# Token rows of a mixture of experts: split once ahead of all pairs of experts, instead of once in every pair

## The reference, cut to what matters

```
u2 = modulate(rmsnorm(h, g_norm2), sh2, sc2)          # 256 x 1024 token rows
comb = weights of the 2 experts (of 32) chosen for each token, zero elsewhere
for e in range(32):
    hid = silu(u2 @ w1[e]) * (u2 @ w3[e])             # 1024 -> 512
    y = y + comb[:, e] * (hid @ w2[e])                # 512 -> 1024
```

## Time and profile before

| | us |
|---|---|
| median of 3 executions | 2202.26 |
| lowest, highest | 2196.2, 2210.37 |
| the profiled execution | 2203.71 |
| its span, first to last instruction | 2201.9 |

### The profile page before, as it was taken

One profiled execution on the slowest core, in us unless ns is written; L12 is line 12 of the kernel. 1 busy time (PEld: TensorE's weight loads), 2 busy tenths in 40 slices (PEclk: granted clock), 3 DMA queues, 4 the chain that ended last, 5 costly groups with the idle time before them and its releaser, 6 DMA issues. The chain is left out here.

```text
span 2201.9 us, 34859 instructions
## 1 busy us (share of the span) xinstructions
PE 2115.3 (96%) x13433; PEld 1839.4 (84%) x13433; DVE 1655.9 (75%) x2247; ACT 1111.8 (50%) x1291; POOL 455.8 (21%) x239
## 2 busy tenths in 40 slices
PE   6999999999999999999999998999979999999996
PEld 6998999559998998999658997999957777777775
DVE  5665887548666765778538655788789999999998
ACT  4343353334433433354324343524348888888885
POOL 8600180809004500081718100000010000000000
PEclk9999999999998999999999999999989999999999
DMA  8854564436655655464336653435649999999994
GB/s 260 267 183 141 158 213 141 143 125 226 211 176 186 232 184 178 145 200 154 134 134 211 199 193 96 153 116 166 235 155 362 369 369 378 364 362 377 367 366 171
DMA packets 238996, 484.33 MB, mean 220 GB/s; under 512 B 10612, under 2 KB 178848, under 8 KB 222528
## 3 DMA queue, kind: packets, MB, share of 16 engines
q1 hardware_dynamic: 226880, 443.58, 57.5%
q0 software_dynamic: 11424, 37.44, 5.1%
q10 hardware_dynamic: 608, 2.14, 0.2%
HBM read 482.03 MB, written 1.09 MB: 219 GB/s over the span
## 5 line engine op out<-in xcount | busy, mean ns | idle before, releaser
L748 PE MATMUL misc<-xh,ring_low 128*128 128x256 f32 x1536 | 427.9, 279 | 0.0
L747 PE MATMUL misc<-xl,high_b 128*128 128x256 f32 x1408 | 394.0, 280 | 9.4 <-DVE xl L2117 6.9
L749 PE MATMUL misc<-xh,high_b 128*128 128x256 f32 x1408 | 392.0, 278 | 0.0
L748 PEld LDWEIGHTS misc<-xh,ring_low 128*128 128x128 f32 x1536 | 291.9, 190 | 3.4
L2779 DVE TENSOR_TENSOR ring_low<-ring,high_b 128x2048 fp32r<-128x2048 f32 x128 | 287.1, 2284 | 0.0
L747 PEld LDWEIGHTS misc<-xl,high_b 128*128 128x128 f32 x1408 | 267.2, 190 | 13.7 <-DVE xl L2117 7.1
L749 PEld LDWEIGHTS misc<-xh,high_b 128*128 128x128 f32 x1408 | 267.0, 190 | 0.0
L2126 DVE TENSOR_TENSOR ring_low<-ring,high_b 128x2048 fp32r<-128x2048 f32 x88 | 226.2, 2611 | 39.7 <-ACT high_b L1613 39.7
L1890 ACT ACTIVATE high_b<-ring 128x2048 fp32r<-128x2048 f32 x124 | 235.7, 1914 | 33.9 <-DMA ring<-in_w_dram 33.0
L1644 ACT ACTIVATE arena<-arena 128x256 f32<-128x256 f32 x88 | 36.8, 418 | 427.7 <-DVE arena L2160 427.7
L1310 PE MATMUL misc<-high_b,ue 128*128 128x512 f32 x512 | 204.2, 399 | 1.9 <-DVE ue L2822 1.2
(11 more groups left out here) (426 smaller groups left out, 4964.1 us busy)
## 6 DMA issues: line engine op xcount, KB each, us to landing
ring<-in_w_dram SPq DMA_DIRECT2D x128, 1024.0 KB, 7.8
ring<-in_w_in_dram SPq DMA_DIRECT2D x72, 1024.0 KB, 5.5
ring_d<-in_w_dram SPq DMA_DIRECT2D x128, 512.0 KB, 5.2
ring<-in_ffn_w_gate_dram SPq DMA_DIRECT2D x44, 1024.0 KB, 5.4
ring<-in_ffn_w_up_dram SPq DMA_DIRECT2D x44, 1024.0 KB, 7.8
ring_d<-in_ffn_w_down_dram SPq DMA_DIRECT2D x88, 512.0 KB, 7.3
arena<-in_w_ada_dram POOLq DMA_DIRECT2D x48, 512.0 KB, 4.4
ring<-in_w_out_dram SPq DMA_DIRECT2D x20, 1024.0 KB, 4.9
```

Source lines behind the costliest of these rows:

```text
L747: pe.matmul(dst, wh, ml, start=start, stop=False, **kw)
L748: pe.matmul(dst, wl, mh, start=False, stop=False, **kw)
L749: return pe.matmul(dst, wh, mh, start=False, stop=stop, **kw)
```

## The change

The rows `u2` are split into `uh` and `ul` (fp32r, in the room of `xh` and `xl`) once ahead of the loop: ACT copies `uh` between its second and third block of weights, DVE subtracts `ul` after the first choice. `sel` becomes fp32r. The gather makes for each group two passes, with `uh` and with `ul` (a pair then has 32 fp32r matmuls of 128 columns), and the two results lie beside each other in one bank of 512 columns, in the order that `ue` has. So a group is moved to `ue` by one copy of 512 columns: for q = 0, 1 by ACT, for q = 2, 3 by DVE, and that copy drains the bank. In a pair's orders, ACT's `high(i + 1, 0, 0)` comes behind `gate3` instead of ahead of the tokens, and DVE has nothing between the `low_d` and `hidden_e` 1. `u2` now lies in the room of `y2`.

```diff
 def gather(i, groups, before=0):                                # PE
-    for q in groups:
-        b = claim3(i, TOKENS[q] - before)
-        for kk in range(2):
-            k = 2 * q + kk
-            for t in range(NT):
-                mm = pe.matmul(b[:, kk * P:(kk + 1) * P], u2[:, t, k * P:(k + 1) * P], sel[:, t, :], ...)
-        mm.then_inc(filled, 1)
+    banks = {}
+    for part_, rows_ in enumerate((uh, ul)):
+        if before and part_ and groups[0] == 0:
+            pe.wait_ge(ul_ready, NT)
+        for q in groups:
+            if not part_:
+                banks[q] = claim3(i, TOKENS[q] - before)
+            b = banks[q].rearrange("p (k h s c) -> p k s h c", k=2, h=2, s=2)
+            for kk in range(2):
+                k = 2 * q + kk
+                for t in range(NT):
+                    mm = pe.matmul(b[:, kk, part_], rows_[:, t, k * P:(k + 1) * P],
+                                   sel[:, t, :].rearrange("p (h c) -> p h c", h=2), ...)
+            if part_:
+                mm.then_inc(filled, 1)
...
 def tokens(i, groups, turn_=0):                                 # ACT
     for q in groups:
         wait_pair_filled(act, i, F_TOKENS[q] if turn_ == 0 else q - 3)
-        act.activation(ue[:, 2 * q:2 * q + 2, :, 0:CAP], bank_of(M0 + TOKENS[q])[:, 0:2 * P]...,
-                       ACT.Copy).then_inc(ue_high, 1)
+        act.activation(ue[:, 2 * q:2 * q + 2, :, :]..., bank_of(M0 + TOKENS[q]),
+                       ACT.Copy).then_inc(drained[(M0 + TOKENS[q]) % 4], 1)
...
 def from_down(i, last):                                         # ACT
     products(i, 1, 7)
+    tokens(i, (0, 1))
+    gate3(i, 1)
     if not last:
         high(i + 1, 0, 0)
-    tokens(i, range(2))
-    gate3(i, 1)
-    tokens(i, range(2, 4))
...
 def tokens(i, groups):                                          # DVE
     for q in groups:
-        dve.wait_ge(ue_high, i * 4 + (4 + q + 1))
-        dve.tensor_tensor(ue[:, 2 * q:2 * q + 2, :, CAP:2 * CAP], bank_of(M0 + j)[:, 0:2 * P]...,
-                          ue[:, 2 * q:2 * q + 2, :, 0:CAP].bitcast(F32), ALU.subtract)...
+        wait_pair_filled(dve, i, F_TOKENS[q])
+        dve.tensor_copy(ue[:, 2 * q:2 * q + 2, :, :]..., bank_of(M0 + TOKENS[q]))\
+            .then_inc(drained[(M0 + TOKENS[q]) % 4], 1)
...
 def pair(i, last):                                              # DVE
     for c in range(CPE):
         low_d(i, 1, c)
-    tokens(i, range(2))
     hidden_e(i, 1)
     if not last:
         low(i + 1, 0, 0)
-    tokens(i, range(2, 4))
+    tokens(i, (2, 3))
...
 # ahead of the loop
+    for t in range(NT):                                         # ACT, between blocks x_ = 1 and 2
+        act.wait_ge(u2_rows, t + 1)
+        act.activation(uh[:, t, :], u2[:, t, :], ACT.Copy).then_inc(uh_ready, 1)
 choose(0)                                                       # DVE
+for t in range(NT):
+    dve.wait_ge(uh_ready, t + 1)
+    dve.tensor_tensor(ul[:, t, :], u2[:, t, :], uh[:, t, :].bitcast(F32), ALU.subtract).then_inc(ul_ready, 1)
 weighing()
 weigh(0, 0)
-tokens(-1, range(1))
 low(0, 0, 0)
-tokens(-1, range(1, 4))
```

More of the change, by code:

```diff
@@ L211, in two_blocks @@
         xh, xl = over("xh", [KD, SEQ]), over("xl", [KD, SEQ])
+        beside(A_X + 2 * KD * SEQ + NT * D)
+        sel = over("sel", [NT, 2 * CAP])
+        A_JOIN = low_at[0]
         beside(ARENA)
@@ L356, in two_blocks @@
         number = route(1)
-        at[0] = A_X
-        u2 = part([NT, D])
-        sel = part([NT, 2 * CAP])
+        at[0] = A_JOIN
+        join = part([CAP])
+        assert at[0] <= A_OSQ
+        u2 = y2
+        uh, ul = (a[:, :, :].rearrange("p a b -> p (a b)").rearrange("p (t d) -> p t d", t=NT) for a in (xh, xl))
+        at[0] = A_HID + 4 * SEQ
         both = part([2, 2 * BLK])
-        join = part([CAP])
-        assert at[0] <= A_X + 2 * KD * SEQ
+        assert at[0] <= A_X
         at[0] = A_OUT
@@ L463, in two_blocks @@
         zeroed = sem("zeroed")
+        u2_rows = sem("u2_rows")
+        uh_ready = sem("uh_ready")
+        ul_ready = sem("ul_ready")
         rt_in = sem("rt_in")
@@ L480, in two_blocks @@
         xh_ready = sem("xh_ready")
-        ue_high = sem("ue_high")
         y_ready = sem("y_ready")
@@ L1291, in gather @@
                 def gather(i, groups, before=0):
-                    for q in groups:
-                        b = claim3(i, TOKENS[q] - before)
-                        for kk in range(2):
-                            k = 2 * q + kk
-                            for t in range(NT):
-                                mm = pe.matmul(b[:, kk * P:(kk + 1) * P], u2[:, t, k * P:(k + 1) * P], sel[:, t, :],
-                                               start=(t == 0), stop=(t == NT - 1))
-                        mm.then_inc(filled, 1)
+                    banks = {}
[10 more added lines that the diff above has]
+                                    mm = pe.matmul(b[:, kk, part_], rows_[:, t, k * P:(k + 1) * P],
+                                                   sel[:, t, :].rearrange("p (h c) -> p h c", h=2),
+                                                   start=(t == 0), stop=(t == NT - 1))
+                            if part_:
+                                mm.then_inc(filled, 1)
                 def gate_up_e(i, half, j):
@@ L1357, in gathered_experts @@
                 pe.wait_ge(sel_ready, 1)
-                gather(0, range(4), 16)
+                pe.wait_ge(uh_ready, NT)
+                gather(0, range(0, 2), 16)
+                gather(0, range(2, 4), 16)
                 pe.wait_ge(zero_ready, 1)
@@ L1926, in tokens @@
                         wait_pair_filled(act, i, F_TOKENS[q] if turn_ == 0 else q - 3)
-                        act.activation(ue[:, 2 * q:2 * q + 2, :, 0:CAP],
-                                       bank_of(M0 + TOKENS[q])[:, 0:2 * P].rearrange("p (a b c) -> p a b c", a=2, b=2),
-                                       ACT.Copy).then_inc(ue_high, 1)
+                        act.activation(ue[:, 2 * q:2 * q + 2, :, :].rearrange("p a b c -> p (a b c)"),
+                                       bank_of(M0 + TOKENS[q]), ACT.Copy).then_inc(drained[(M0 + TOKENS[q]) % 4], 1)
                 def first_weights(i, part_):
@@ L2035, in _ @@
             for x_ in range(4):
+                if x_ == 2:
+                    for t in range(NT):
+                        act.wait_ge(u2_rows, t + 1)
+                        act.activation(uh[:, t, :], u2[:, t, :], ACT.Copy).then_inc(uh_ready, 1)
                 n = RING["moe"] + x_
@@ L2740, in token_rows @@
                 dve.wait_ge(gained, t + 1)
-                link(dve.scalar_tensor_tensor(out=token(t), in0=token(t), scalar=rstd[:, t:t + 1],
-                                              in1=by_part(shrow), op0=ALU.mult, op1=ALU.add))
+                dve.scalar_tensor_tensor(out=token(t), in0=token(t), scalar=rstd[:, t:t + 1],
+                                         in1=by_part(shrow), op0=ALU.mult, op1=ALU.add).then_inc(u2_rows, 1)
             def placing():
@@ L2766, in choose @@
                 def choose(e):
-                    dve.tensor_tensor(by_half(sel), iota.unsqueeze(1).unsqueeze(1).to_broadcast([P, NT, 2, CAP]),
+                    dve.tensor_tensor(by_half(sel[:, :, :]), iota.unsqueeze(1).unsqueeze(1).to_broadcast([P, NT, 2, CAP]),
                                       both_of(place, e), ALU.is_equal).then_inc(sel_ready, 1)
@@ L2773, in weigh @@
                     dve.wait_ge(sel_ready, i + 1)
-                    dve.tensor_tensor(by_half(selw), by_half(sel), both_of(comb, e), ALU.mult).then_inc(selw_ready, 1)
+                    dve.tensor_tensor(by_half(selw), by_half(sel[:, :, :].bitcast(F32)), both_of(comb, e), ALU.mult).then_inc(selw_ready, 1)
                 def low(i, half, x):
@@ L2819, in tokens @@
                     for q in groups:
-                        dve.wait_ge(ue_high, i * 4 + (4 + q + 1))
[L2821 to L2825, removed]
+                        wait_pair_filled(dve, i, F_TOKENS[q])
+                        dve.tensor_copy(ue[:, 2 * q:2 * q + 2, :, :].rearrange("p a b c -> p (a b c)"),
+                                        bank_of(M0 + TOKENS[q])).then_inc(drained[(M0 + TOKENS[q]) % 4], 1)
                 def first_weights(i, outs_of=None):
@@ L2859, in gathered_experts @@
                 choose(0)
+                for t in range(NT):
+                    dve.wait_ge(uh_ready, t + 1)
+                    dve.tensor_tensor(ul[:, t, :], u2[:, t, :], uh[:, t, :].bitcast(F32), ALU.subtract)\
+                        .then_inc(ul_ready, 1)
                 weighing()
                 weigh(0, 0)
-                tokens(-1, range(1))
                 low(0, 0, 0)
-                tokens(-1, range(1, 4))
                 for j in (-5, -2, -1):
@@ L2908, in experts @@
                 dve.nop().then_inc(sel_ready, 1)
+                dve.wait_ge(uh_ready, NT)
+                wait_filled(dve, FILL["moe"] + 3)
```

## The result

The changed kernel takes 2221.68 us in the median of 6 executions (2216.59 to 2230.7), the kernel before 2202.95 (2196.2 to 2210.37): a ratio of 1.0085, with a 95% interval of 1.0063 to 1.0108. That is 19 us more; the forecast was 2217.

What follows compares the result with a forecast made beforehand. DVE was taken to set the turn, PE close behind. 14.5 us over 15 turns plus 0.5 ahead of the loop put 2203.7 at 2218.7; the median stands 1.45 lower, giving 2217, range 2194 to 2246.

Steps and rivals of the forecast that it cites:

- What sets the turn: In the pair loop, DVE sets the turn with PE on its heels; third low ready at 1880.04, fourth slot about 1880.1.
- The gather on PE: Each fp32r matmul of 128 columns in the gather costs 0.11 us, nothing gained or lost; bounds 0.054 and 0.222.
- the cheap: Rival, 15%: the gather's narrow matmul streams freely at 0.054 us; a turn of 34.17, in all 2203.
- slow rival: Rival, 20%: the gather's narrow matmul costs 0.222 us, like a float32 one; 36.8 a turn, in all 2245.
- DVE's work: Per turn on DVE, four subtractions (1.33 us) go and two PSUM copies (1.20) come: balance -0.13 us.
- The wait for the gate: DVE stands ahead of hidden_e 1, from 1868.70 to 1869.18, until ACT's gate; some 0.5 us a turn.
- The wait for the high: DVE waits 0.76 us ahead of the next pair's first low, until ACT's high, now behind gate3, ends.
- The turns: A loop turn becomes 35.07 us, 0.97 above the mean of 34.10, paid in 15 turns: 14.5 us.
- The signs: Profile after: DVE idle at two places 15 times, no PE wait for hidden_e 1, waits for low parts in slots 2 to 4.
- Ahead of the loop: Splitting the rows once and the first gather delay PE's first slot: +0.5 us, between 0 and 2.
- The rival on the other side: Rival, 20%: PE sets the turn, DVE's idle time costs nothing, PE's lost wait of 0.33 gains 5 us: 2197.
- The sum: Loop 14.5 plus 0.5 ahead of it makes 15 us on the profiled execution's 2203.7: 2218.7, as a median 2217.

Runs made afterwards that it cites:

- the first two experiments: Changed kernel with ACT's high(i + 1, 0, 0) back ahead of the tokens: 1.0038; kernel before with that line moved behind gate3: 1.0030; ratios to the kernel before.
- the first exchange: Against the changed kernel: DVE copies q = 0, 1, ACT q = 2, 3, ACT's high(i + 1, 0, 0) ahead of all; ratio 1.0077 to the kernel before.
- the second: Against the changed kernel: DVE copies q = 1, 3, ACT q = 0, 2, ACT's high(i + 1, 0, 0) ahead of all; ratio 1.0000 to the kernel before.
- the kernel with one line back: Changed kernel with ACT's high(i + 1, 0, 0) moved back ahead of the tokens q = 0, 1; ratio 1.0038 to the kernel before.

## Why the prediction was right

- **What sets the turn** was DVE, without slack between its third low and PE's fourth slot. Right: in the changed kernel the slot starts at 1900.19 and the low part is there at 1900.13, and taking the waits from DVE gave the time back. With them gone the chain runs through PE and the turn is only 0.17 below the one before, so PE was indeed on DVE's heels.
- **The gather on PE**: 0.11 for a matmul was forecast, between 0.054 and 0.222; it is 0.108. Neither the cheap nor the slow rival came. It is the cost of the 64-column records, as forecast. The Trainium skill's figure for matmuls of 128 columns in a stream of weight loads and matmuls ("TensorE: Matmul & The Clock Gate", section "Back-to-back issue gap"), about 81 ns, isn't what the trace shows, and the measurement decides.
- **DVE's work**: 1.20 for two copies, as forecast.
- **The wait for the gate**: 0.40 measured, 0.48 forecast. **The wait for the high**: 0.59 measured, 0.76 forecast. The prediction let each wait begin where the next instruction had begun before, 0.07 to 0.10 ahead of the recorded end; an instruction that has to wait does not overlap in this way, so DVE is through with `low_d` at 1868.78 and not 1868.70, and 1869.18 - 1868.78 = 0.40. `hidden_e` takes 1.21 and not 1.11 by the same slip, and the other 0.07 is that ACT's high let the low start 1.80 us after the start of `hidden_e` and not 1.87. Together with the rest the three lows come 1.05 later; 1.10 was forecast, the turn 35.03 against 35.07.
- **The turns**: 12.9 us more over 15 turns in the profiles (525.7 against 512.9 us), 14.5 forecast. The larger part of the difference is the first turn, 35.41 before and 35.29 after; it lies outside the 14 turns from which the forecast took its 34.10, and was counted with 0.97 more. The late loads of the kernel before are not to be seen after: the other 14 turns are all within 35.02 to 35.06.
- **The signs.** PE's wait for `hidden_e` 1 is gone, but for 0.2 us a turn at this place that the profile puts down to no engine. Its waits for low parts are at the third and the fourth slot, and not at the second as well.
- **Ahead of the loop** the size was off: 0.5 forecast, 28.85 - 27.07 = 1.8 measured, near the upper bound of 2. The prediction had taken 24 of the gather's records at 0.19 us, by the earlier trace rows, and nothing for the clock. The granted clock of these stretches, before (two rows) and after (two rows):

```profile
1627.00:1633.00 6.00, 5.99 (x32) 5.85 (x32) 5.11 (x12) 1.15 (x3) 0.00 (x0) 0.61 0.02 4
1634.00:1638.00 4.00, 3.73 (x16) 2.85 (x16) 4.00 (x2) 3.26 (x4) 0.00 (x0) 1.00 0.18 27
```

```profile
1639.00:1646.00 7.00, 6.66 (x30) 6.47 (x31) 6.75 (x12) 4.10 (x5) 0.00 (x0) 0.50 0.01 4
1647.00:1651.00 4.00, 3.33 (x8) 2.66 (x9) 4.00 (x3) 4.00 (x5) 0.00 (x0) 0.50 0.00 0
```

  Both gathers start after 4.6 us in which PE did nothing. During the float32 one the clock rose to 2.4 GHz; the fp32r one ran at 1.2 GHz throughout (its records 0.21 to 0.22 us each), and the first eight matmuls of `gate_up_e` behind it did as well:

```profile
1647.67 0.79 PE L1325 MATMUL misc<-high_b,ue 128*128 128x512 f32 x1 [0.98 <-ACT ue L1944]
1648.26 0.63 PE L1327 MATMUL misc<-ring_low,ue 128*128 128x512 f32 x1
...
1651.18 0.39 PE L1325 MATMUL misc<-high_b,ue 128*128 128x512 f32 x1
```

  Those eight take 1651.18 - 1647.67 = 3.51 us; in the kernel before it was 1.93, from 1634.27 to

```profile
1636.20 0.49 PE L1310 MATMUL misc<-high_b,ue 128*128 128x512 f32 x1
```

  A part of these 1.6 us is won back behind them, where PE had to wait for a low part before.

- **The rival on the other side** (DVE's gaps cost nothing, PE's wait is gone) is refuted by the first two experiments.
- **The sum** is closer than its terms: 15 forecast against 14.6 from the router on, because the loop was forecast 1.6 too high and the stretch ahead of it 1.3 too low. That this cancels is luck.
- What the median has beyond the 14.6 us of the profiles, some 4 us, is within the interval of the measurement, and no experiment assigned it.

## What to carry to other kernels

Where PE, DVE and the DMA engines are all at 96 to 99%, the question about a change is not what work it saves but what each engine has to do in the moment it would have to wait: here one `high` moved behind a wait cost 0.5 us a turn in either kernel, and copies taken out of DVE's way left it standing. Walk one turn row by row, with the order of the change, on the engine without slack; that gave the turn to 0.04 us. And when work is moved to fill a gap, look which bank, which queue and which reader stand behind it: the first exchange failed on all three, and the second, of the same size, brought everything back.

## What was not expected of the hardware

TensorE's clock inside the loop. The kernel before and the changed one hold the full granted clock from turn to turn. With the copies exchanged, PE waits 0.23 us in the gather and 0.43 behind it, and in three of the turns the matmuls that follow run at 1.2 GHz, half speed:

```profile
1908.18 0.52 PE L1351 MATMUL misc<-ring_d_low,hidl 128*128 128x512 f32 x1 [0.43 <-DVE hidl L2823]
1908.51 0.62 PE L1352 MATMUL misc<-high_r,hidl 128*128 128x512 f32 x1
```

```profile
1900.00:1912.00 12.00, 11.34 (x66) 9.89 (x67) 11.73 (x13) 9.85 (x10) 0.00 (x0) 0.86 0.86 353
1909.00:1911.00 2.00, 2.00 (x6) 1.58 (x5) 1.80 (x2) 2.00 (x2) 0.00 (x0) 0.50 0.26 107
1912.00:1920.00 8.00, 8.00 (x37) 6.58 (x36) 6.36 (x6) 6.57 (x8) 0.00 (x0) 1.00 0.93 322
```

Each such turn is 35.97 to 36.00 us instead of 34.6, 1.4 more. What PE did just before was the narrow fp32r matmuls, the float32 joining and two short waits. But the same work and the same waits (0.23 to 0.26 and 0.43 us) stand in all 15 turns, and in 12 of them the clock stayed. One turn of the kernel with one line back had it too (35.95), after a wait of 0.73 ahead of `down_e` 1 and none in the gather; three other turns there had waits of 0.72 or 0.73 and kept the clock. The version with q = 1, 3 on DVE, with one wait of about 0.3, had it in none of 15 turns. What decides it no run shows.
